# A hybrid decoder trunk: three of four input turns made token-stationary, their result and the queries and keys turned through a scratch in HBM

## The reference, cut to what matters

```python
def _rglru_mixer(x, w_in, conv_w, conv_b, ..., w_out):
    gate, u = jnp.split(x @ w_in, 2, axis=-1)              # 2048 -> 2 x 2048
    u = conv_general_dilated(u, conv_w, ...) + conv_b      # depthwise over positions, width 4
    r = sigmoid(block_diag(u) @ gate_a_w + gate_a_b)       # 8 blocks of 256
    i = sigmoid(block_diag(u) @ gate_x_w + gate_x_b)
    log_a = -8 * r * softplus(-lam); a = exp(log_a)
    h = associative_scan(a, u * i * sqrt(-expm1(2 * log_a)))
    return (gelu(gate) * h) @ w_out
# attention: q, k, v = x @ w_qkv; rotary on 32 of 128 channels; softmax(q k / sqrt(128)) v, then w_out
# each sub-layer: x = LayerNorm(alpha * x + y); MLP: relu(x @ w1)**2 @ w2
```

## Time and profile before

| what | value |
|---|---|
| median of the runs (3) | 2084.79 us |
| time of the profiled execution | 2084.47 us |
| span of its profile | 2082.7 us |
| granted TensorE clock | 1.00 of full speed |
| busy: PE, DVE, ACT | 100%, 61%, 47% of the span |
| moved by DMA | 447.13 MB, mean 215 GB/s |

### The profile page before, as it was taken

One profiled execution on the slowest core, in us unless ns is written; L12 is line 12 of the kernel. 1 busy time (PEld: TensorE's weight loads), 2 busy tenths in 40 slices (PEclk: granted clock), 3 DMA queues, 4 the chain that ended last, 5 costly groups with the idle time before them and its releaser, 6 DMA issues.

```text
span 2082.7 us, 27784 instructions
## 1 busy us (share of the span) xinstructions
PE 2075.3 (100%) x9566; PEld 1730.7 (83%) x9566; DVE 1268.0 (61%) x1247; ACT 969.6 (47%) x1164; POOL 21.3 (1%) x16
## 2 busy tenths in 40 slices
PE   9999999999999999999999999999999999999999
PEld 8898888888888888888888888888888888888887
DVE  6869666665554565555756565775655555555565
ACT  5596455443444443443644444454434434444442
POOL 0000010000000000000100000010000000000000
PEclk9999999999999999999999999999999999999999
DMA  7565758766766766776566667667667766766763
GB/s 258 194 202 189 234 181 258 247 203 201 241 220 185 241 224 202 212 240 191 179 210 203 211 218 234 200 206 250 222 212 212 241 205 208 236 218 224 241 213 121
DMA packets 243003, 447.13 MB, mean 215 GB/s; under 512 B 18400, under 2 KB 47328, under 8 KB 241888
## 3 DMA queue, kind: packets, MB, share of 16 engines
q1 hardware_dynamic: 237008, 436.73, 66.3%
q10 hardware_dynamic: 5904, 9.18, 1.4%
HBM read 419.63 MB, written 18.87 MB: 211 GB/s over the span
## 4 chain that ended last, share of the span: by engine, by line
PE 97%; DVE 1%; ACT 1%; issue 1%; DMA 0%; SPq 0%; DVEq 0%; ACTq 0%
PE ps L465 88%; PE ps L456 4%; PE ps L453 2%; PE ps L598 1%; DVE gate L1134 0%; PE ps L636 0%; PE ps L645 0%; DVE wl L1055 0%; DMA f<-in_x_dram 0%; ACT wh L759 0%; ACT gate L803 0%; PE ps L563 0%; PE ps L564 0%; PE ps L565 0%; DVE hid L1142 0%
## 5 line engine op out<-in xcount | busy, mean ns | idle before, releaser
L1055 DVE TENSOR_TENSOR wl<-wst,wh 128x1024 fp32r<-128x1024 f32 x742 | 886.4, 1219 | 373.6 <-ACT wh L759 370.9
L759 ACT ACTIVATE wh<-wst 128x1024 fp32r<-128x1024 f32 x742 | 770.2, 1059 | 686.5 <-PE ps L465 407.1
L465 PE MATMUL ps<-wh,xin 128*128 128x512 f32 x2816 | 756.1, 390 | 0.0
L465 PE MATMUL ps<-wh,hid 128*128 128x512 f32 x2560 | 695.8, 390 | 0.0
L465 PEld LDWEIGHTS ps<-wh,xin 128*128 128x128 f32 x2816 | 527.8, 188 | 108.8
L465 PEld LDWEIGHTS ps<-wh,hid 128*128 128x128 f32 x2560 | 479.5, 188 | 98.7
L465 PE MATMUL ps<-wl,xin 128*128 128x512 f32 x1408 | 433.5, 389 | 0.0
L465 PE MATMUL ps<-wl,hid 128*128 128x512 f32 x1280 | 404.6, 389 | 0.0
L465 PEld LDWEIGHTS ps<-wl,xin 128*128 128x128 f32 x1408 | 264.3, 188 | 54.9
L465 PEld LDWEIGHTS ps<-wl,hid 128*128 128x128 f32 x1280 | 240.3, 188 | 50.0
L456 PE MATMUL ps<-xin,wh 128*128 128x512 f32 x512 | 177.0, 396 | 0.0
(11 more groups left out here) (123 smaller groups left out, 562.9 us busy)
## 6 DMA issues: line engine op xcount, KB each, us to landing
wst<-in_mlp_w_dram SPq DMA_DIRECT2D x512, 512.0 KB, 4.8
wst<-in_moba_w_qkv_dram SPq DMA_DIRECT2D x96, 512.0 KB, 4.8
wst<-in_rg_w_in_dram SPq DMA_DIRECT2D x62, 512.0 KB, 4.4
wst<-in_rg_w_out_dram SPq DMA_DIRECT2D x32, 512.0 KB, 4.9
sq_by_quad<-f SPq DMA_DIRECT2D x128, 128.0 KB, 2.6
f<-sq_by_quad SPq DMA_DIRECT2D x32, 512.0 KB, 4.9
wst<-in_moba_w_out_dram SPq DMA_DIRECT2D x32, 512.0 KB, 4.9
f<-in_x_dram SPq DMA_DIRECT2D x8, 256.0 KB, 6.9
```

The costliest lines, as they stand in the source:

```text
L465: return pe.matmul(dst, src[:, c, part, a * P:(a + 1) * P], (wl if low else wh)[:, s, w], start=(c == 0 and part + low == 0), stop=(c == N ...
L759: act.activation(wh[:, off % SPLITS, :], wst[:, slot, :], ACT.Copy).then_inc(wh_done, 1)
L1055: dve.tensor_tensor(wl[:, off % SPLITS, :], wst[:, off % STAGE, :], wh[:, off % SPLITS, :], ALU.subtract).then_inc(wl_done, 1)
```

## The change

1. Turns 0 to 2 of `u` become token-stationary, into banks 0-1, 2-3 and 0-1. ACT evicts each (`take_u`, 2 instructions), SP stores it to `sq_by_quad` with 4 DMAs and reads it back with one (`u_through`), and DVE transposes it into `u3` (`turn_u`). The store of turn t stands ahead of the third load of turn t+2 in SP's program, the read ahead of the fourth; for t = 2 these are the gate blocks. `turn_u` stands behind the split of offset 11 of the next turn (`U_TURN` = 5), and `conv_start` behind the same one on ACT. Turn 3 stays as it was. Turn 2 waits for `psum_free` 1, which is now `turn_u(0)`; `psum_free` 3 is now `turn_u(2)`.
2. `conv_hi_part` goes from the middle of the turn's splits to behind the eviction, ahead of offset 14; `conv_lo` goes behind offset 14.
3. The first input pair is transposed and split by chunks of 128 rows, so that the first matmuls need one chunk; the second pair is transposed behind the first chunk's matmuls.
4. Queries and keys go through the scratch too: 4 stores behind the rotation and one read, all by SP; ACT issues none.
5. The last of the output's pieces is computed and stored in halves.

```diff
+U_TOKEN = NG - 1
+U_TURN = 5
...
+            def u_through(t):
+                def store():
+                    sp.wait_ge(u_evict, HALVES * (t + 1))
+                    for i in range(GROUP):
+                        sp.dma_start(to_quad[i], u_out[i * 32:(i + 1) * 32, :, :]).then_inc(u_stored, 16)
+                def back():
+                    sp.wait_ge(u_stored, (t + 1) * (16 * GROUP))
+                    sp.dma_start(u_quad, by_quad.rearrange("p (i n) -> p i n", i=GROUP)).then_inc(u_back, 16)
+                return {2: store, 3: back}
-            with sp.Fori(1, NG) as t:
-                load_turn(w_in, D + t * COLS, B_U + t * BLOCKS)
+            for t in range(1, NG):
+                load_turn(w_in, D + t * COLS, B_U + t * BLOCKS, u_through(t - 2) if t >= 2 else {})
             for gb in range(BLOCKS):
+                if gb in (2, 3):
+                    u_through(U_TOKEN - 1)[gb]()
...
-                sp.wait_ge(qk_evict, HALVES * (2 * g + part + 1))
...
+            def store_qk(g, part):
+                sp.wait_ge(qk_rotated, 2 * g + part + 1)
+                for i in range(GROUP):
+                    sp.dma_start(to_quad[i], qk_out[i * 32:(i + 1) * 32, :, :]).then_inc(qk_stored, 16)
+            def read_qk(g, part):
+                sp.wait_ge(qk_stored, (2 * g + part + 1) * (16 * GROUP))
                 if 2 * g + part:
                     sp.wait_ge(qk_ready, 2 * g + part)
+                sp.dma_start(qk_quad, by_quad.rearrange("p (i n) -> p i n", i=GROUP)).then_inc(qk_back, 16)
...
-            input_pair(1)
-            between = {k - 1: lambda k=k: input_pair(k) for k in range(2, BLOCKS)}
-            turn(xin, 0, B_U, R_X, {**between, BLOCKS - 1: parameters}, halved=True)
+            for kb in range(BLOCKS):
+                if kb == BLOCKS - 1:
+                    parameters()
+                elif kb:
+                    input_pair(kb + 1)
...
+                for c in range(kb * KCH, (kb + 1) * KCH):
+                    if c == 1:
+                        input_pair(1)
+                        pe.wait_ge(pair_ready, R_X + 1)
...
+                    for part, low in ((0, 0), (1, 0), (0, 1)):
+                        for a in range(HALVES):
+                            mm = token_step(xin, 0, a, c, part, low)
+                mm.then_inc(mm_done, 1)
+            token_turn(xin, 2, B_U + BLOCKS, R_X)
+            pe.wait_ge(psum_free, T_U + 1)
+            token_turn(xin, 0, B_U + 2 * BLOCKS, R_X)
             pe.wait_ge(prm_ready, 1)
-            turn(xin, 1, B_U + BLOCKS, R_X)
-            pair(xin, B_U + 2 * BLOCKS, R_X, T_U + 2)
+            turn(xin, 1, B_U + 3 * BLOCKS, R_X)
...
+                splits(b, t, AHEAD if t else BLOCKS, AHEAD + U_TURN)
...
                 if t:
-                    splits(b, t, AHEAD, AHEAD + 1)
                     conv_start(t - 1)
...
+                splits(b, t, AHEAD + U_TURN, LATE)
+                if t < U_TOKEN:
+                    take_u(t, b)
+                else:
+                    take_hl(1, b, u3[:, t * GROUP:(t + 1) * GROUP, :], hl_copied)
+                if t:
                     conv_hi_part(t - 1)
                 splits(b, t, LATE)
...
-                for dst, src in part_moves(qk_quad, qk_out, (2, 3), range(1, GROUP)):
-                    act.dma_start(dst, src).then_inc(qk_moved, 16)
...
+            def turn_u(t):
+                dve.wait_ge(u_back, 16 * (t + 1))
+                dve.transpose(u3[:, t * GROUP:(t + 1) * GROUP, :]..., u_quad...).then_inc(psum_free, 1)
...
+                        for cols in out_pieces(h, g):
+                            dve.scalar_tensor_tensor(out=res[:, h, cols], in0=res[:, h, cols],
+                                                     scalar=rstd[:, h:h + 1], in1=bias_row[:, cols],
+                                                     op0=ALU.mult, op1=ALU.add).then_inc(out_done, 1)
```

More of the change, by code:

```diff
@@ L245, in xt_bank, with out_pieces, first_xt @@
             return ps[:, 4 + k % 4, :].rearrange("p (c t) -> p c t", t=T)
+        def out_pieces(h, g):
+            n = 2 if h == HALVES - 1 and g == NG - 1 else 1
+            return [slice(c, c + COLS // n) for c in range(g * COLS, (g + 1) * COLS, COLS // n)]
+        def first_xt(q):
+            return ps[:, 4 + 3 * q, 0:T]
         def cols_of(w, first):
@@ L382, in _ @@
             for g in range(NG):
-                k_before = {2: lambda: move_qk(g - 1, 1)} if g else {}
+                k_before = move_qk(g - 1, 1) if g else {}
                 p_before = {3: lambda: move_p(g - 1)} if g else {}
-                for part, also in enumerate((k_before, p_before, {2: lambda: move_qk(g, 0)})):
+                for part, also in enumerate((k_before, p_before, move_qk(g, 0))):
                     load_turn(moba_w_qkv[0], part * D + g * COLS, B_QKV + (3 * g + part) * BLOCKS, also)
@@ L398, in _ @@
                 for g in range(1, NG):
[L399 to L402 removed]
+                    for n, cols in enumerate(out_pieces(h, g)):
+                        sp.wait_ge(out_done, h * (NG - 1) + g + n)
+                        sp.dma_start(out[0, h * P:(h + 1) * P, cols], res[:, h, cols]).then_inc(stored, 16)
+            sp.wait_ge(stored, 16 * (HALVES * NG + 1))
         @block.gpsimd
@@ L431, in _, with turn @@
             by_twos = [(n, low) for m in range(0, GROUP, 2) for low in range(2) for n in (m, m + 1)]
-            def turn(src, half, b, ready, between={}, halved=False):
+            def turn(src, half, b, ready):
                 dst = banks(half)
                 for kb in range(BLOCKS):
-                    if kb in between:
-                        between[kb]()
                     pe.wait_ge(pair_ready, ready + (kb + 1))
-                    if halved and kb < 2:
-                        pe.wait_ge(first_lo[kb], 1)
-                    else:
-                        pe.wait_ge(wl_done, b + kb + 1)
+                    pe.wait_ge(wl_done, b + kb + 1)
                     for c in range(kb * KCH, (kb + 1) * KCH):
-                        if halved and c in (1, 3):
-                            pe.wait_ge(wl_done, kb + 1)
                         s = c // KCH % SPLITS
@@ L499, in last_token_turn @@
                         mm.then_inc(ln_half, 1)
-            def pair(src, b, ready, free):
-                for j in range(2):
-                    pe.wait_ge(psum_free, free + (j - 1))
-                    turn(src, j, b + j * BLOCKS, ready)
             def input_pair(k):
@@ L805, in conv_start, with take_u @@
                 ins.then_inc(conv_begun, 1)
+            def take_u(t, b):
+                act.wait_ge(mm_done, b + BLOCKS)
+                if t:
+                    act.wait_ge(psum_free, T_U + t)
+                for a in range(HALVES):
+                    by_part = u_out.rearrange("p q (c a r) -> p a c q r", c=GROUP, a=HALVES)[:, a]
+                    by_col = ps[:, 2 * (t % 2) + a, :].rearrange("p (c q r) -> p c q r", c=GROUP, q=GROUP)
+                    act.activation(by_part, by_col, ACT.Copy).then_inc(u_evict, 1)
             for t in range(NG):
                 b = B_U + t * BLOCKS
+                splits(b, t, AHEAD if t else BLOCKS, AHEAD + U_TURN)
+                if t == 1:
+                    act.wait_ge(sp_abs, 1)
+                    act.activation(small[:, 1, :], small[:, 0, :], ACT.Exp, scale=-1.0).then_inc(sp_exp, 1)
                 if t:
-                    splits(b, t, AHEAD, AHEAD + 1)
                     conv_start(t - 1)
-                    splits(b, t, AHEAD + 1, AHEAD + CONV)
-                    if t == 1:
-                        act.wait_ge(sp_abs, 1)
-                        act.activation(small[:, 1, :], small[:, 0, :], ACT.Exp, scale=-1.0).then_inc(sp_exp, 1)
+                splits(b, t, AHEAD + U_TURN, LATE)
+                if t < U_TOKEN:
+                    take_u(t, b)
+                else:
+                    take_hl(1, b, u3[:, t * GROUP:(t + 1) * GROUP, :], hl_copied)
+                if t:
                     conv_hi_part(t - 1)
-                splits(b, t, AHEAD + CONV if t else BLOCKS, LATE)
-                take_hl(t % 2, b, u3[:, t * GROUP:(t + 1) * GROUP, :], hl_copied)
                 splits(b, t, LATE)
```

97 lines of the change are left out of this document (61 added, 36 removed).

## The result

| | before | after |
|---|---|---|
| median of the runs | 2084.64 us (5 runs) | 2097.24 us (5 runs, 2096.63 to 2099.16) |
| profiled execution, its span | 2084.47, 2082.7 us | 2099.16, 2097.4 us |
| busy: PE | 2075.3 us | 2079.8 us |

The changed kernel is slower by 0.6%: ratio 1.0063, 95% interval 1.0051 to 1.0074. The profiled execution is the longest of its five, 1.9 us above the median; the other four have spans of 2094.8 to 2096.2 us.

What follows compares the result with a forecast made beforehand. PE bounds the kernel, but ACT's and DVE's chain would set gate product 2's start: +12.8 - 0.1 = +12.7 on the profiled 2084.47 gives 2097.2, plus 0.3 for the median, 2097.5 us; range 2093.5 to 2103.5.

Steps and rivals of the forecast that it cites:

- PE's matmul savings: Turns 1 to 3 of u: three turns at 22.20 - 21.76 = 0.44 save PE 1.3 us, which buys nothing.
- The ring: Turns of u, from the end of one `turn_u` to the next: 24.7 us against PE's turn of 21.76.
- The load of offset 11, taken as 4.9: Fourth load in each turn of u, behind the third load and the read: 4.9 us, landing at 21.2.
- Where the ring starts: First round trip, turn 0's result: `turn_u(0)` was to end at 54.9 us.
- the last lands 2.6 later: about 45.3: First trip's four stores: 1.77 us to issue, the last landing 2.6 later, at about 45.3.
- The waits: PE waits 0.7 at turn 2, then 5.4, 5.9 and 2.6 us at gate products 0, 1 and 2.
- Product 2's start: Gate product 2 waits for the sigmoids of product 0 and starts at 124.4 instead of 111.62: +12.8 us.
- the low half of block 1 that the prediction had named as a bound: Start-up: PE waiting for the first low half of block 1 was the bound of 0.5 us lost.
- the gain of 0.2: Start-up: first matmul no longer needs the second pair's transposition; gain 0.2 us, from 0.5 gained to 0.5 lost.
- Queries and keys, the end: Attention: trip hidden by a cover of 5.8 us, cost 0. Output's end: halves gain 0.1 us.
- the 0.1 gained: End of the output: last piece in halves gains 0.1 us, from 0.4 gained to 0.6 lost.
- Rival A: Turns of u: the round trip is hidden and the kernel gets faster, 2082.9 us; chance 0.10.

Runs made afterwards that it cites:

- high_part_late: The changed kernel with ACT's high part of the convolution behind the split of offset 14 instead of ahead of it; 2093.24 us, ratio 1.0039.
- no_trip: The changed kernel without u's scratch stores and reads, the transposition taking the evicted result directly (u's values not the reference's); 2092.00 us, ratio 1.0037.
- reordered_sp: The changed kernel with the same operations and trips, but another order on ACT, DVE and SP in the turns of u; 2083.14 us, ratio 0.9993.
- the reordered kernels: Two versions of the changed kernel with other orders in the turns of u, trips issued by SP (2083.14 us) or by POOL (2083.04 us).
- read_first: The changed kernel with SP's store ahead of the second load and its read ahead of the third; 2096.78 us, ratio 1.0059.
- One_turn: The changed kernel with only turn 0 token-stationary and sent through the scratch, turns 1 to 3 as before; 2091.53 us, ratio 1.0033.

## Why the prediction was right, and where it was off

- **Where the loss is.** Right: all of it ahead of gate product 2, PE's matmul savings buying nothing. Forecast +12.7, measured +12.6 by the medians, +14.7 in the profiled span.
- **The ring.** 24.7 us worked out, 25.0 and 24.2 in the trace. high_part_late and no_trip made it shorter, the first by 2.4 and 1.0 where its parts say 2.1 each, the second by 1.8 and 0.6 where the read's share was put at 0.8 each. The load of offset 11, taken as 4.9, took 5.52 and 4.76.
- **Where the ring starts.** Off by 2.1: `turn_u(0)` ends at 57.0, forecast 54.9. The step that failed is "the last lands 2.6 later: about 45.3". It took 6.16. So SP issued the read at 48.84 and the load behind it at 49.23, 3.5 later than worked out; this load was then faster (4.30, forecast 5.7). The median over a whole kernel was the wrong row for this place: the twelve stores in the turns of u took 3.4 to 6.2, median 4.0. What made this one the longest was not tested; the DMA moved 249 GB/s while it was under way, against 217 over the span.
- **The waits.** Forecast 0.7, 5.4, 5.9, 2.6; measured 1.8, 4.6, 3.9 and none. The last two were displaced by a term that the prediction put at nothing, the fall of the clock behind a wait: product 0 took 7.5 us instead of 5.76 and product 1 8.6, of which the clock's part is 1.5 and 2.5. Product 1 ended at 126.2 and the sigmoids, forecast for 124.4, at 125.8, so PE had no wait left to show. Of the clock's 4.0 us in this execution only the last 0.4 counted; the rest lay in the shadow of ACT's and DVE's chain. The time of the forecast came out right for the chain, not because the waits did.
- **The price of a wait.** Product 2's start was forecast at 124.4 and was 126.2 in the profile: 1.9 from the third transposition, late because the ring started late, less 0.5 along the chain behind it, plus the 0.4.
- **The start of the kernel.** The first real matmul came at 6.86, as forecast; but turn 0 then took 26.5 us (turn 1 starts at 33.33) instead of 25.3, with a wait of 0.3 at 11.48 for the low half of block 1 that the prediction had named as a bound, so the gain of 0.2 was a loss of about 0.3 here and a gain of 0.1 in reordered_sp. Inside the bound.
- **Queries and keys, the end.** No wait of PE in the attention. The last store of ACT leaves at 2093.54 and the span ends 3.9 later, 3.7 before: the 0.1 gained isn't there.
- **Rival A.** As a forecast for this order it was wrong. Its time, 2082.9, is that of the reordered kernels. The Trainium skill, "DMA: Bandwidth & Descriptors", section "Rules for kernel authors", says to issue a DMA early and wait for it late. In the changed kernel the order broke this: SP's wait for the store stood ahead of a load that the ring needed, and ACT and DVE held splits, and so further loads, behind the convolution. With the splits ahead of it the trace of reordered_sp agrees with the rule, and the trip costs PE no wait.

## What to carry to other kernels

Before work is added between two engines that run in program order, follow one whole turn from a result to the same result of the next turn, through the loads that each split releases; if that ring is longer than the bounding engine's turn, its length and not the operation's price is the cost. Then look for an order that lets what releases loads go first, before giving the change up. Price a long wait of PE at its length and the slow matmuls behind it, and ask whether something hides these.

## What the runs showed of the hardware

- After every wait of PE of 3.5 to 6.1 us in these traces (13 of them) 12 to 27 matmuls of 256 columns ran at 1.2 GHz, 0.2135 us apart instead of 0.12: 1.1 to 2.5 us. The number doesn't follow the length of the wait: 27 behind one of 3.9 us, 17 behind one of 5.4. After the eight waits of 0.9 to 1.8 us there was none. After the one of 2.1 us (read_first, turn 2) the clock fell too, about 1.2 us after PE had started again, and about 1.6 us were lost in its matmuls of 512 columns; they lay ahead of the next wait. Filling a wait with matmuls took the slow ones away (product 2 in 5.84 us instead of 8.55).

```profile
58.20:61.00 2.80, 2.80 (x8) 2.16 (x7) 1.21 (x2) 2.80 (x5) 0.00 (x0) 0.50 0.22 83
```

- Kernels with such long waits scatter more, for a reason that no run here tests. One_turn's spans run from 2087.8 to 2091.3, those of the reordered kernels from 2080.7 to 2081.9. But the kernel before has no such wait, and one group of 15 of its executions runs from 2083.57 to 2086.84.
- The twelve stores of 128 KB in the turns of u took 3.4 to 6.2 us to land (median 4.0), against 2.6 as the median of the kernel's 172.
